# A transformer block on one core: the out-projection and the first two up tiles of the feed-forward, computed in two passes over halves of the tokens

## The chip, the cores and the metric

One core of a Trainium2 chip runs the kernel. The metric is the device time of one execution in microseconds (us); what is given for a kernel is the median of several runs. The core has five engines that run side by side, each through its own list of instructions in order: TensorE (PE, matmuls; PEld are its weight loads), VectorE (DVE), ScalarE (ACT), GpSimd (POOL) and SyncE (SP, which here issues only DMAs). Engines wait for each other by semaphores.

## The reference

Two blocks on a sequence of 1024 tokens of width 1024, all in float32. The part around the change is the end of the first block's mixer and the start of its feed-forward:

```python
mix = jnp.concatenate([attn, rw.astype(x.dtype)], axis=-1) @ w_out[l]
x = x + rms_norm(mix, norm_mix_post[l])
f = conv_gated_ffn(rms_norm(x, norm_ffn_pre[l]), w_ffn_up[l], conv_w[l], conv_b[l], w_ffn_down[l])
x = x + rms_norm(f, norm_ffn_post[l])

def conv_gated_ffn(h, w_up, conv_w, conv_b, w_down):      # w_up: 1024 x 8192, w_down: 4096 x 1024
    u = h @ w_up
    u_pad = jnp.pad(u, ((0, 0), (CONV_WIDTH - 1, 0), (0, 0)))
    u = conv_b + sum(conv_w[j] * u_pad[:, j:j + S] for j in range(CONV_WIDTH))
    gate, val = jnp.split(u, 2, axis=-1)
    return (jax.nn.gelu(gate, approximate=True) * val) @ w_down
```

`rms_norm` divides each token by the root of the mean of its squares over the 1024 channels. So the norm of a token needs all eight channel tiles of the product before it, and two such norms stand one behind the other between the out-projection and the first product of the feed-forward.

## The kernel before

Everything is held with channels on the 128 partitions and tokens along the free axis: a full activation is eight tiles of 128 x 1024 (`KT` = 8, `T` = 1024). A product with a weight tile of 1024 x 128 is `gemm` (line 481): for each of eight k it does three products (high part of the weight by high part of the activation, high by low, low by high), and each of these for both halves of 512 tokens, `hs=(0, 1)`: 48 matmuls of 128x512, into the PSUM banks `2 * u` and `2 * u + 1`. Weight tiles go through two buffers: SP loads tile g into `w_raw`, POOL splits it (`split`, L397 and L400) into `w_hi` and `w_lo` as soon as product g - 2 is done, and PE waits for it (`w_split`).

The out-projection is eight such products (L879 to L887). ACT copies each result to `y1` and squares it; DVE adds the squares in pairs (`norm_pair`), PE sums them over the channels (`norm_part`, L526, matmuls with one output column), ACT takes the root, DVE the reciprocal (`norm_inverse`), and PE spreads it over the partitions (`norm_sum`, L540). DVE then adds the scaled `y1` to the residual `x1`, channel tile by channel tile, ACT squares `x1`, and the second norm runs in the same way. Its result, times a gain, is split into `x_hi` (ACT) and `x_lo` (DVE) by `apply_all`, and the up products of the feed-forward wait for `x_lo` tile by tile (`parts`). Both norms are over all 1024 tokens at once. After them DVE zeroes `f_acc` (L2003), to which the down products of each of the feed-forward's groups are added.

Later, around the feed-forward's own norms, the same kernel already works by halves: `down(h, k)` and `head_tile(h, k)` call `gemm` with `hs=(h,)` (24 matmuls), and `half_sums` (L503), `half_spread` (L511), `half_pair` and `half_inverse` do a norm of 512 tokens. Their rows are shown below.

Nearly every operation of ACT and DVE is issued by the helper at L114, so its line tells little and the names of the tiles have to be read. In the trace digits are cut from the names: `y` is `y1` (or `y2`), `x` is `x1` (or `x2`, `x3`), `x_in` at 1750 us and later is the reloaded `x1`. The order of the work is written out by hand; no scheduler moves it.

## Time and profile before

| | us |
|---|---|
| median of 3 runs | 2678.81 (2676.87 to 2682.08) |
| the profiled execution's own time | 2673.34 |
| its span | 2671.5 |
| PE busy | 2514.2 (94% of the span) |
| DVE busy | 1202.5 (45%) |
| POOL busy | 870.2 (33%) |
| ACT busy | 689.2 (26%) |

The span runs from the first to the last instruction of the profiled execution. Busy times are sums over stages, and 94% on PE says that what can be gained is where PE stands still; that has to be looked up stretch by stretch.

### The profile page before, as it was taken

The page shows a single profiled execution, that of the slowest core. Times are in us where ns is not written, and L with a number is a line of the kernel's source. Part 1 is how long each engine was busy: PE and PEld are TensorE (multiplying, and loading weights), DVE is VectorE, ACT ScalarE, POOL GpSimd, SP SyncE. Part 2 cuts the span into 40 slices and gives each one's busy share as a digit, 9 for nine tenths or more (in the row PEclk, how much of TensorE's full clock was granted, in tenths as well). Part 3 has the DMA queues.
Part 4 walks back from the last instruction along what each step waited for, and adds up shares of the span by engine and source line. Part 5 has one row for each costly group of instructions (what it writes and reads, how often), then busy time and mean ns, then how long its engine had stood idle before and what let it go on. Part 6 is the DMA issues. An engine that isn't in the chain of part 4 may idle for free.

```text
span 2671.5 us, 45354 instructions
## 1 busy us (share of the span) xinstructions
PE 2514.2 (94%) x18246; PEld 2008.6 (75%) x18246; DVE 1202.5 (45%) x1588; ACT 689.2 (26%) x1035; POOL 870.2 (33%) x498
## 2 busy tenths in 40 slices
PE   8999889999879999999999999999979999988897
PEld 6777589986658888888888888877768777733576
DVE  4477766644273422342233223335350666544252
ACT  3233433331222200220022002212332233255521
POOL 3322000011313333344333333465654455400021
PEclk9999989999879999999999999999989999989797
DMA  4211000002122211221122111143311111220021
GB/s 146 70 33 39 22 3 5 4 19 87 40 80 73 75 55 55 72 77 47 63 71 77 48 47 47 47 142 104 128 60 40 50 47 49 75 79 1 0 89 69
DMA packets 44352, 155.98 MB, mean 58 GB/s; under 512 B 4264, under 2 KB 6568, under 8 KB 43688
## 3 DMA queue, kind: packets, MB, share of 16 engines
q1 hardware_dynamic: 26784, 97.53, 11.2%
q10 hardware_dynamic: 17416, 56.31, 6.0%
q8 instruction: 110, 1.80, 0.3%
q14 instruction: 42, 0.34, 0.0%
HBM read 133.37 MB, written 20.45 MB: 58 GB/s over the span
## 4 chain that ended last, share of the span: by engine, by line
PE 83%; DVE 8%; ACT 4%; issue 2%; POOL 1%; DVEq 1%; DMA 0%; ACTq 0%; POOLq 0%
PE ps L493 51%; PE ps L1018 5%; PE ps L598 5%; PE ps L1041 2%; ACT ab L114 2%; DVE proj L114 2%; PE ps L1118 1%; PE ps L762 1%; PE ps L772 1%; DVE x_lo L114 1%; PE ps L547 1%; PE ps L769 1%; DVE nrm_a L114 1%; DVEq L103 1%; PE ps L1138 1%
## 5 line engine op out<-in xcount | busy, mean ns | idle before, releaser
L397 POOL TENSOR_TENSOR w_hi<-w_raw,small 128x1024 fp32r<-128x1024 f32 x178 | 339.3, 1906 | 1494.5 <-PE ps L493 1137.3
L493 PE MATMUL ps<-x_hi,w_hi 128*128 128x512 f32 x1600 | 512.0, 394 | 31.5 <-DVE x_lo L114 15.7
L493 PE MATMUL ps<-x_lo,w_hi 128*128 128x512 f32 x1600 | 507.5, 391 | 0.0
L493 PE MATMUL ps<-x_hi,w_lo 128*128 128x512 f32 x1600 | 507.3, 391 | 0.0
L400 POOL TENSOR_TENSOR w_lo<-w_raw,w_hi 128x1024 fp32r<-128x1024 f32 x178 | 436.4, 2452 | 13.9
L493 PEld LDWEIGHTS ps<-x_hi,w_hi 128*128 128x128 f32 x1600 | 300.2, 189 | 102.4 <-issue 18.5
L493 PEld LDWEIGHTS ps<-x_hi,w_lo 128*128 128x128 f32 x1600 | 302.1, 189 | 63.7
L493 PEld LDWEIGHTS ps<-x_lo,w_hi 128*128 128x128 f32 x1600 | 302.4, 189 | 62.9
L114 DVE SCALAR_TENSOR_TENSOR cv<-ps,cst,cv 128x1023 f32<-128x1023 f32 x64 | 82.1, 1283 | 256.2 <-ACT cv L114 250.8
L493 PE MATMUL ps<-f_hi,w_hi 128*128 128x512 f32 x512 | 170.1, 393 | 3.8 <-POOL w_lo L400 3.8
L493 PE MATMUL ps<-f_hi,w_lo 128*128 128x512 f32 x512 | 168.8, 391 | 0.0
L493 PE MATMUL ps<-f_lo,w_hi 128*128 128x512 f32 x512 | 168.8, 391 | 0.0
L114 DVE TENSOR_TENSOR f_acc<-f_acc,ps 128x1024 f32 (+1 forms) x40 | 40.3, 1008 | 252.7 <-PE ps L493 251.0
L114 ACT ACTIVATE cg<-ps,cst 128x1024 f32<-128x1024 f32 x32 | 38.7, 1210 | 394.3 <-PE ps L493 394.3
L114 DVE SCALAR_TENSOR_TENSOR cg<-ps,cst,cg 128x1023 f32<-128x1023 f32 x64 | 82.1, 1282 | 110.8 <-ACT cg L114 105.0
L114 ACT ACTIVATE cv<-ps,cst 128x1024 f32<-128x1024 f32 x32 | 38.7, 1209 | 306.7 <-PE ps L493 306.7
L493 PEld LDWEIGHTS ps<-f_hi,w_hi 128*128 128x128 f32 x512 | 96.6, 189 | 24.2 <-POOL w_lo L400 4.4
L493 PEld LDWEIGHTS ps<-f_hi,w_lo 128*128 128x128 f32 x512 | 96.5, 189 | 20.4
L493 PEld LDWEIGHTS ps<-f_lo,w_hi 128*128 128x128 f32 x512 | 96.4, 188 | 19.8
L598 PE MATMUL ps<-x_hi,w_hi 128*128 128x512 f32 x224 | 90.7, 405 | 2.7 <-DVE raw L114 2.6
L114 DVE TENSOR_TENSOR zz<-proj,e 128x256 f32<-128x256 f32 x112 | 70.2, 626 | 40.2 <-ACT e L114 28.6
L598 PE MATMUL ps<-x_lo,w_hi 128*128 128x512 f32 x224 | 88.0, 393 | 0.0
(290 smaller groups left out, 3822.0 us busy)
## 6 DMA issues: line engine op xcount, KB each, us to landing
w_raw<-wall SPq DMA_DIRECT2D x178, 512.0 KB, 3.5
ada_w<-wada ACTq DMA_DIRECT2D x24, 512.0 KB, 3.5
fill_spill<-stage ACTq DMA_DIRECT2D x24, 256.0 KB, 2.0
x_in<-xT ACTq DMA_DIRECT2D x8, 512.0 KB, 8.4
x<-xT ACTq DMA_DIRECT2D x1, 4096.0 KB, 12.5
x_spill<-x ACTq DMA_DIRECT2D x1, 4096.0 KB, 11.1
x_in<-x_spill ACTq DMA_DIRECT2D x2, 2048.0 KB, 12.6
x_spill<-x ACTq DMA_DIRECT2D x2, 2048.0 KB, 8.3
```

The source lines that it names most:

```text
L103: self.eng.drain()
L114: return emit(*args, **kw)
L397: nc.gpsimd.tensor_tensor(w_hi[:, u, :, :], w_raw[:, u, :, :], sm["one"].unsqueeze(2).to_broadcast([P, KT, P]), ALU.mult).then_inc(S("w_hi ...
L400: nc.gpsimd.tensor_tensor(w_lo[:, u, :, :], w_raw[:, u, :, :], w_hi[:, u, :, :].bitcast(F32), ALU.subtract).then_inc(S("w_split"), 1)
L493: last = mm(ps[:, 2 * u + h, :], w[:, u, k, :], x[:, k, h * 512:(h + 1) * 512], start=(k == 0 and w is w_hi and x is hi), stop=(k == KT - ...
L547: last = mm(ps[:, b + h, :], w[:, u, k, :], x[:, k, h * 512:(h + 1) * 512], start=(k == 0 and w is w_hi and x is x_hi), stop=(k == KT - 1 ...
L598: last = mm(ps[:, 7, :], w[:, g % 2, k, :], x[:, k, h * 512:(h + 1) * 512], start=(k == 0 and w is w_hi and x is x_hi), stop=(k == KT - 1 ...
L762: last = mm(ps[q, 4 + p, m * RC:(m + 1) * RC], m1[q, r, m, 0:RC], xx[q, r, 0, m, :], start=True, stop=True)
L769: mm(ps[q, 4 + p, m * RC:(m + 1) * RC], xx[q, r, 1, m, :], y_sb[q, p, m, :], start=True, stop=True)
L772: last = mm(ps[q, 4 + p, 256 + m * RC:256 + (m + 1) * RC], y_sb[q, p, m, :], xx[q, r, 1, m, :], start=True, stop=True)
L1018: last = mm(ps[:, 7, :], w[:, g % 2, k, :], x[:, k, h * 512:(h + 1) * 512], start=(k == 0 and w is w_hi and x is x_hi), stop=(k == KT - 1 ...
L1041: i_ = mm(ps[0:r, 2 * (l % 2) + h % 2, (h // 2) * n:(h // 2 + 1) * n], lh, rh, start=True, stop=True)
```

## The change

The out-projection's eight products become sixteen of 24 matmuls: first all eight channel tiles for tokens 0 to 511, then all eight for tokens 512 to 1023 (`out_half`). For this SP loads the eight tiles of `w_out` a second time and POOL splits them a second time (positions 28 to 35; the feed-forward starts at position 36). The two norms between out-projection and feed-forward are done per half, with the helpers that the later stage already used; the norms of half 0 are placed in PE's order between the products of the second pass. The first two up products (the first gate and the first value tile) are also done by halves: `up_half(0, 0)` and `up_half(0, 1)` before the last sums of half 1's norms, `up_half(1, 0)` and `up_half(1, 1)` behind them. Both halves use the same split weights. The spill of `x1` to memory is two DMAs, one per half. The zeroing of `f_acc` goes, and the first group's down products are copied into it instead of added; for that the first group stands outside the loop on PE and DVE. The later stages change in semaphore counts only.

```diff
-G_IN, G_OUT, G_FFN = 0, 20, 28
+G_IN, G_OUT, G_FFN = 0, 20, 36
+W_FFN = G_OUT + KT
 FFN_GROUPS, GROUP = 4, 8
-W_IN2 = G_FFN + FFN_GROUPS * 3 * GROUP
+W_IN2 = W_FFN + FFN_GROUPS * 3 * GROUP
...
+        sq_m = at("sq_m", [P, 2, T], 38)
+        pairs_m = at("pairs_m", [P, 2, T], 40)
...
-            return sq_l[:, k // 2 % 2, :] if lane == "a" else sq_r[:, k // 2 % 2, hc(i % 2)]
+            return sq_l[:, k // 2 % 2, :] if lane == "a" else (sq_m if i < 2 else sq_r)[:, k // 2 % 2, hc(i % 2)]
         def half_pairs(lane, i, j):
-            return pairs_l[:, j % 2, :] if lane == "a" else pairs_a[:, j % 2, hc(i % 2)]
+            return pairs_l[:, j % 2, :] if lane == "a" else (pairs_m if i < 2 else pairs_a)[:, j % 2, hc(i % 2)]
...
-            with sp.Fori(G_OUT // 2, G_LAST // 2) as i:
-                for u in range(2):
-                    g = sp.snap(2 * i + u)
-                    src = dr["wall"][bass.ds(g, 1)]
-                    sp.wait_ge(S("w_split"), 2 * i + u - 1)
-                    load(src, u).then_inc(S(f"w_in{u}"), 16)
+            for lo, hi, back in ((G_OUT, G_OUT + KT, 0), (G_OUT + KT, G_LAST, KT)):
+                with sp.Fori(lo // 2, hi // 2) as i:
+                    for u in range(2):
+                        g = sp.snap(2 * i + u - back)
+                        src = dr["wall"][bass.ds(g, 1)]
+                        sp.wait_ge(S("w_split"), 2 * i + u - 1)
+                        load(src, u).then_inc(S(f"w_in{u}"), 16)
...
-                if k1 == KT:
+                if k1 == KT and whole:
...
+            def out_half(h, k, k0=0, k1=KT):
+                g = G_OUT + KT * h + k
+                gemm(g, g % 2, x_hi, x_lo, parts=("x_lo_done", 8) if h == k == 0 else None, hs=(h,), k0=k0, k1=k1)
+            def up_half(h, u, k0=0, k1=KT):
+                gemm(G_FFN + u, u, x_hi, x_lo, parts=("x_lo_done", 16 + 8 * h), hs=(h,), k0=k0, k1=k1, whole=(h == 1))
             pe.wait_ge(S("inv_used"), 4)
-            gemm(G_OUT, 0, x_hi, x_lo, parts=("x_lo_done", 8))
+            out_half(0, 0)
             pe.wait_ge(S("bonus_used"), 4)
-            gemm(G_OUT + 1, 1, x_hi, x_lo)
-            for k in range(2, KT):
-                gemm(G_OUT + k, k % 2, x_hi, x_lo)
-                if k % 2:
-                    norm_part(1, (k - 3) // 2)
-            norm_sum(1, 3)
-            norm_sum(2)
-            def ffn_up(gr):
-                with pe.Fori(0, GROUP) as j:
+            for k in range(1, KT):
+                out_half(0, k)
+                if k in (2, 4, 6):
+                    half_sums("a", 0, k // 2 - 1)
+            out_half(1, 0, 0, 4)
+            half_sums("a", 0, 3)
+            out_half(1, 0, 4)
+            half_spread("a", 0)
+            out_half(1, 1)
+            half_sums("b", 0, 0)
+            out_half(1, 2)
+            half_sums("b", 0, 1)
+            half_sums("a", 1, 0)
+            out_half(1, 3, 0, 3)
+            half_sums("b", 0, 2)
+            out_half(1, 3, 3)
+            half_sums("b", 0, 3)
+            out_half(1, 4, 0, 3)
+            half_spread("b", 0)
+            out_half(1, 4, 3)
+            out_half(1, 5)
+            half_sums("a", 1, 1)
+            out_half(1, 6)
+            out_half(1, 7, 0, 4)
+            half_sums("a", 1, 2)
+            out_half(1, 7, 4)
+            up_half(0, 0, 0, 4)
+            half_sums("a", 1, 3)
+            up_half(0, 0, 4)
+            half_spread("a", 1)
+            up_half(0, 1)
+            for j in range(KT // 2):
+                half_sums("b", 1, j)
+            half_spread("b", 1)
+            for u in range(2):
+                up_half(1, u)
+            def ffn_up(gr, first=0):
+                with pe.Fori(first, GROUP) as j:
                     g = pe.snap(3 * GROUP * gr + G_FFN + 2 * j)
                     for u in range(2):
...
+            def ffn_down(gr):
...
+            ffn_up(0, 1)
+            ffn_down(0)
+            with pe.Fori(1, FFN_GROUPS - 1) as gr:
+                ffn_up(gr)
+                ffn_down(gr)
...
+            eng.preload_act_table_set("sqrt_and_others")
...
+            def mixed(h, k):
+                g = G_OUT + KT * h + k
+                act.wait_ge(S("gemm_mm"), g + 1)
+                copy(y1[:, k, hc(h)], ps[:, 2 * (g % 2) + h, :]).then_inc(S("gemm_evac"), 1)
+                half_square("a", h, k, y1[:, k, hc(h)])
+            def x1_square(h, k):
+                act.wait_ge(S("res_done"), KT * h + k + 1)
+                half_square("b", h, k, x1[:, k, hc(h)])
+            def x1_spill(h):
+                act.dma_start(x1_dram.rearrange("p (k t) -> p k t", t=T)[:, :, hc(h)], x1[:, :, hc(h)]).then_inc(S("x1_out"), 16)
+            def scaled_high(h, k):
+                act.wait_ge(S("h_done"), 8 * h + k + 1)
+                copy(x_hi[:, k, hc(h)], scaled_bank(h, k)).then_inc(S("x_hi_done"), 1)
             for k in range(KT):
-                g = G_OUT + k
-                act.wait_ge(S("gemm_mm"), g + 1)
-                copy(y1[:, k, :], pair(2 * (g % 2))).then_inc(S("gemm_evac"), 1)
-                act.wait_ge(S("norm_pair"), 4 + k // 2)
-                fn(sq_of[1][:, k % 2, :], y1[:, k, :], ACT.Square).then_inc(S("norm_sq"), 1)
-            root(1)
-            norm(2, lambda k: x1[:, k, :], lambda k: act.wait_ge(S("res_done"), k + 1))
-            act.dma_start(x1_dram, x1[:, :, :].rearrange("p k t -> p (k t)")).then_inc(S("x1_out"), 16)
-            high(1, lambda k: nrm_a[:, k % 2, :], "h_done")
-            act.wait_ge(S("x1_out"), 16)
+                mixed(0, k)
+            half_root("a", 0)
+            for i in range(KT):
+                for k in ((), (0, 1, 2), (3, 4, 5), (6, 7), (), (), (), ())[i]:
+                    x1_square(0, k)
+                if i == 3:
+                    x1_spill(0)
+                if i == 4:
+                    half_root("b", 0)
+                for k in ((), (), (), (), (0, 1, 2), (3, 4, 5, 6), (7,), ())[i]:
+                    scaled_high(0, k)
+                mixed(1, i)
+            half_root("a", 1)
+            for k in range(KT):
+                x1_square(1, k)
+            x1_spill(1)
+            half_root("b", 1)
+            for k in range(KT):
+                scaled_high(1, k)
+            act.wait_ge(S("x1_out"), 32)
...
-            for j in range(4):
-                norm_pair(1, j)
-            norm_inverse(1)
-            dve.wait_ge(*landed("x_again"))
-            for k in range(KT):
-                stt(nrm_a[:, k % 2, :], y1[:, k, :], par("g_mix_post", k, 1), rs_of(1), ALU.mult, ALU.mult)
-                tt(x1[:, k, :], x1[:, k, :], nrm_a[:, k % 2, :], ALU.add).then_inc(S("res_done"), 1)
-                if k >= 2 and k % 2 == 0:
-                    norm_pair(2, k // 2 - 1)
-            norm_pair(2, 3)
-            apply_all(2, 2, nrm_a, lambda k: x1[:, k, :], lambda k: par("g_ffn_pre", k, 1))
-            memset(f_acc[:, 0:8, :], 0.0)
...
+            def mix_residual(h, k):
+                stt(step_bank(h), y1[:, k, hc(h)], par("g_mix_post", k, 1), half_bank("a", h), ALU.mult, ALU.mult)
+                tt(x1[:, k, hc(h)], x1[:, k, hc(h)], step_bank(h), ALU.add).then_inc(S("res_done"), 1)
+            def scaled_up(h, k):
+                stt(scaled_bank(h, k), x1[:, k, hc(h)], par("g_ffn_pre", k, 1), half_bank("b", h),
+                    ALU.mult, ALU.mult).then_inc(S("h_done"), 1)
+            def scaled_low(h, k):
+                dve.wait_ge(S("x_hi_done"), 16 + 8 * h + k + 1)
+                tt(x_lo[:, k, hc(h)], scaled_bank(h, k), x_hi[:, k, hc(h)].bitcast(F32), ALU.subtract)\
+                    .then_inc(S("x_lo_done"), 1)
+            for h in range(2):
+                for j in range(3 if h else 0, 4):
+                    half_pair("a", h, j)
+                half_inverse("a", h)
+                if h == 0:
+                    dve.wait_ge(*landed("x_again"))
+                dve.wait_ge(S("half_bc_a"), h + 1)
+                for k in range(KT):
+                    mix_residual(h, k)
+                    if k in (2, 4, 6):
+                        half_pair("b", h, k // 2 - 1)
+                    if h == 0 and k == 5:
+                        half_pair("a", 1, 0)
+                half_pair("b", h, 3)
+                half_inverse("b", h)
+                dve.wait_ge(S("half_bc_b"), h + 1)
+                for k in range(KT):
+                    scaled_up(h, k)
+                    if k:
+                        scaled_low(h, k - 1)
+                    if h == 0 and k == 3:
+                        half_pair("a", 1, 1)
+                scaled_low(h, KT - 1)
+                if h == 0:
+                    half_pair("a", 1, 2)
...
-            with dve.Fori(0, FFN_GROUPS - 1) as gr:
+            def ffn_group(gr, first=False):
                 memset(pair(4), 0.0)
...
-                        tt(f, f, pair(2 * u), ALU.add).then_inc(S("gemm_evac"), 1)
+                        i_ = vcopy(f, pair(2 * u)) if first else tt(f, f, pair(2 * u), ALU.add)
+                        i_.then_inc(S("gemm_evac"), 1)
...
+            ffn_group(0, first=True)
+            with dve.Fori(1, FFN_GROUPS - 1) as gr:
+                ffn_group(gr)
```

What stands on each engine at the places that matter, as the programs list it. On PE, before, between the last product of the out-projection (its last rows) and the first up product; `pairs_141` and `pairs_140` hold the pair sums of the first and the second norm:

```order
L493 MATMUL ps<-x_lo,w_hi 128x512 x2
L493 MATMUL ps<-x_hi,w_lo 128x512 x2
L526 MATMUL ps<-cst,pairs_141 128x1 [waits norm_pair]
L526 MATMUL ps<-cst,pairs_141 128x1 x7
L526 MATMUL ps<-cst,pairs_141 128x1 [waits norm_pair]
L526 MATMUL ps<-cst,pairs_141 128x1 x7
L540 MATMUL ps<-cst,small 128x128 [waits norm_inv]
L540 MATMUL ps<-cst,small 128x128 x7
L526 MATMUL ps<-cst,pairs_140 128x1 [waits norm_pair]
L526 MATMUL ps<-cst,pairs_140 128x1 x7
```

On PE now, in the second pass, around the end of its third and the start of its fourth product (`pairs_m` holds the pair sums of half 0's second norm, `pairs_l` those of the first norms):

```order
L497 MATMUL ps<-x_hi,w_lo 128x512
L507 MATMUL ps<-cst,pairs_m 128x1 [waits half_pair_b]
L507 MATMUL ps<-cst,pairs_m 128x1 x3
L507 MATMUL ps<-cst,pairs_l 128x1 [waits half_pair_a]
L507 MATMUL ps<-cst,pairs_l 128x1 x3
L497 MATMUL ps<-x_hi,w_hi 128x512 [waits gemm_evac,w_split]
L497 MATMUL ps<-x_lo,w_hi 128x512
L497 MATMUL ps<-x_hi,w_lo 128x512
```

The sums of the norms have moved from behind the product of all eight tiles to between products of the second pass, and each still waits for DVE's pair sum. The end of half 1's second norm, with the first up product of half 1 behind it, reads on PE:

```order
L507 MATMUL ps<-cst,pairs_m 128x1 [waits half_pair_b]
L507 MATMUL ps<-cst,pairs_m 128x1 x3
L515 MATMUL ps<-cst,small 128x128 [waits half_inv_b]
L515 MATMUL ps<-cst,small 128x128 x3
L497 MATMUL ps<-x_hi,w_hi 128x512 [waits x_lo_done,gemm_evac,w_split]
L497 MATMUL ps<-x_lo,w_hi 128x512
L497 MATMUL ps<-x_hi,w_lo 128x512
L497 MATMUL ps<-x_hi,w_hi 128x512 [waits x_lo_done]
```

Here PE has nothing left to do but these rows: what it did without a norm has been put ahead of them.

On DVE, before, where the first norm's reciprocal leads into the residual:

```order
L114 RECIPROCAL small<-small 128x8 [waits norm_root]
L114 SCALAR_TENSOR_TENSOR nrm_a<-y_100,cst,ps 128x1024 [waits in_a,norm_bc]
L114 TENSOR_TENSOR x_101<-x_101,nrm_a 128x1024
L114 SCALAR_TENSOR_TENSOR nrm_a<-y_100,cst,ps 128x1024
L114 TENSOR_TENSOR x_101<-x_101,nrm_a 128x1024
```

The same place on DVE now, of half 1:

```order
L115 RECIPROCAL small<-small 128x4 [waits half_root_a]
L115 SCALAR_TENSOR_TENSOR ps<-y_102,cst,ps 128x512 [waits half_bc_a]
L115 TENSOR_TENSOR x_103<-x_103,ps 128x512
L115 SCALAR_TENSOR_TENSOR ps<-y_102,cst,ps 128x512
L115 TENSOR_TENSOR x_103<-x_103,ps 128x512
```

The operations are half as wide, there are twice as many, and the step between the two of a pair lies in PSUM (`ps`) instead of SBUF (`nrm_a`).

## Rows read from the trace of the kernel before

**Rows 1.** The page: the span, and section 1 (busy us, share, instructions).

```profile
span 2671.5 us, 45354 instructions
PE 2514.2 (94%) x18246; PEld 2008.6 (75%) x18246; DVE 1202.5 (45%) x1588; ACT 689.2 (26%) x1035; POOL 870.2 (33%) x498
```

**Rows 2.** Stretches: from:to, length, PE, PEld, DVE, ACT, POOL busy; PEclk, DMA, GB/s.

```profile
624.50:715.60 91.10, 91.08 (x419) 75.97 (x419) 16.19 (x8) 17.20 (x18) 30.06 (x14) 1.00 0.24 87
715.60:765.30 49.70, 23.43 (x111) 22.12 (x111) 32.48 (x27) 14.46 (x15) 4.23 (x2) 0.54 0.16 63
765.30:770.60 5.30, 5.27 (x12) 3.64 (x12) 4.98 (x4) 2.12 (x2) 0.00 (x0) 0.50 0.70 300
796.00:1746.00 950.00, 949.71 (x4200) 786.11 (x4200) 314.44 (x252) 145.17 (x129) 374.35 (x175) 1.00 0.19 61
1757.00:1793.00 36.00, 36.00 (x176) 30.22 (x175) 6.98 (x11) 3.98 (x7) 25.71 (x12) 1.00 0.31 98
```

**Rows 3.** Timeline of PE, 755 to 796: start, duration, what, [idle before <- releaser].

```profile
755.03 3.57 PE L526 MATMUL ps<-cst,pairs 128*128 128x1 f32 x16 [1.45 <-DVE pairs L114]
759.20 1.97 PE L540 MATMUL ps<-cst,small 128*128 128x128 f32 x8 [0.60 <-DVE small L114]
765.33 1.19 PE L493 MATMUL ps<-x_hi,w_hi 128*128 128x512 f32 x2 [4.16 <-DVE x_lo L114]
...
796.01 0.74 PE L493 MATMUL ps<-x_hi,w_hi 128*128 128x512 f32 x2 [0.73 <-DVE cg L114]
```

**Rows 4.** Timeline of PE in the half-width stage: sums, and spread.

```profile
1762.17 0.95 PE L503 MATMUL ps<-cst,pairs_l 128*128 128x1 f32 x8
...
1793.18 0.60 PE L511 MATMUL ps<-cst,small 128*128 128x128 f32 x4
```

**Rows 5.** Timeline of DVE in the half-width stage.

```profile
1762.37 0.69 DVE L114 TENSOR_TENSOR f_acc<-f_acc,ps 128x512 f32<-128x512 f32 x1 [3.97 <-PE ps L493]
1768.76 0.69 DVE L114 TENSOR_TENSOR f_acc<-f_acc,ps 128x512 f32<-128x512 f32 x1 [5.71 <-PE ps L493]
...
1793.45 0.69 DVE L114 TENSOR_TENSOR f_acc<-f_acc,ps 128x512 f32<-128x512 f32 x1 [2.48 <-PE ps L493]
...
1799.29 0.69 DVE L114 TENSOR_TENSOR f_acc<-f_acc,ps 128x512 f32<-128x512 f32 x1 [1.55 <-PE ps L493]
...
1857.42 0.76 DVE L114 SCALAR_TENSOR_TENSOR ps<-f_acc,cst,ps 128x512 f32<-128x512 f32 x1 [3.53 <-PE ps L511]
1858.26 0.69 DVE L114 TENSOR_TENSOR x<-x_in,ps 128x512 f32<-128x512 f32 x1
1859.04 0.76 DVE L114 SCALAR_TENSOR_TENSOR ps<-f_acc,cst,ps 128x512 f32<-128x512 f32 x1
```

**Rows 6.** Timeline of DVE, 628 to 785.

```profile
628.54 2.54 DVE L114 TENSOR_TENSOR x_lo<-proj,x_hi 128x1024 fp32r<-128x1024 f32 x2
...
717.77 3.31 DVE L114 TENSOR_TENSOR pairs<-sq_a 128x1024 f32<-128x1024 f32 x1 [20.24 <-ACT sq_a L114]
...
763.96 1.22 DVE L114 TENSOR_TENSOR x_lo<-nrm_a,x_hi 128x1024 fp32r<-128x1024 f32 x1
...
766.64 1.22 DVE L114 TENSOR_TENSOR x_lo<-nrm_a,x_hi 128x1024 fp32r<-128x1024 f32 x1
...
784.47 6.88 DVE L114 MEMSET f_acc<- 128x8192 f32 x1 [1.83 <-issue]
```

**Rows 7.** Timeline of ACT in the half-width stage: an eviction, a square.

```profile
1864.25 0.60 ACT L114 ACTIVATE proj<-ps 128x512 f32<-128x512 f32 x1 [3.06 <-PE ps L493]
...
1866.50 0.63 ACT L114 ACTIVATE sq_r<-x 128x512 f32<-128x512 f32 x1
```

**Rows 8.** Timeline of POOL: a split after the out-projection, one in the half-width stage.

```profile
717.66 2.34 POOL L400 TENSOR_TENSOR w_lo<-w_raw,w_hi 128x1024 fp32r<-128x1024 f32 x1
...
1774.31 1.90 POOL L397 TENSOR_TENSOR w_hi<-w_raw,small 128x1024 fp32r<-128x1024 f32 x1 [1.13 <-PE ps L493]
1776.28 2.39 POOL L400 TENSOR_TENSOR w_lo<-w_raw,w_hi 128x1024 fp32r<-128x1024 f32 x1
```

**Rows 9.** Tile `w_raw`, 1740 to 1762, beside two reloads of 2 MB each: its DMAs.

```profile
DMA to landing us min/median/max: 3.5/6.3/6.8
```

More of the change, by code:

```diff
@@ L46 @@
 N_POS = G_OUT2 + KT
-WALL_OF = (2 * [G_LAST + k for k in range(KT)] + 2 * [W_IN2 + i for i in IN2_ORDER[:N_HEAD]]
+WALL_OF = (2 * [W_IN2 - KT + k for k in range(KT)] + 2 * [W_IN2 + i for i in IN2_ORDER[:N_HEAD]]
            + [W_IN2 + i for i in IN2_ORDER[N_HEAD:]] + [W_OUT2 + k for k in range(KT)])
@@ L479, in _, with gemm @@
             turned = nc.tensor.transpose
-            def gemm(g, u, hi, lo, first=False, parts=None, hs=(0, 1), k0=0, k1=KT):
+            def gemm(g, u, hi, lo, first=False, parts=None, hs=(0, 1), k0=0, k1=KT, whole=True):
                 if k0 == 0:
@@ L532, in norm_part, with norm_sum @@
                 last.then_inc(S("norm_mm"), 1)
-            def norm_sum(n, done=0):
-                for j in range(done, KT // 2):
+            def norm_sum(n):
+                for j in range(KT // 2):
                     norm_part(n, j)
@@ new lines, in _ @@
+            out_half(1, 5)
[9 more added lines that the diff above has]
+            up_half(0, 1)
+            for j in range(KT // 2):
+                half_sums("b", 1, j)
+            half_spread("b", 1)
+            for u in range(2):
+                up_half(1, u)
@@ L914, in head_tile @@
                 g = G_IN2 + N_HEAD * h + k
[L915 removed]
+                gemm(g, g % 2, x_hi, x_lo, parts=("x_lo_done", 32 + 8 * h) if k == 0 else None, hs=(h,), k0=k0, k1=k1)
             down(0, 0, 0, 7)
@@ L951, in _ @@
             head_tile(0, 1, 0, 1)
-            half_sums("a", 1, 3)
+            half_sums("a", 3, 3)
             head_tile(0, 1, 1, 6)
-            half_spread("a", 1)
+            half_spread("a", 3)
             head_tile(0, 1, 6)
@@ L1169, in _ @@
             g0 = G_OUT2
-            gemm(g0, g0 % 2, x_hi, x_lo, parts=("x_lo_done", 40))
+            gemm(g0, g0 % 2, x_hi, x_lo, parts=("x_lo_done", 48))
             gemm(g0 + 1, (g0 + 1) % 2, x_hi, x_lo)
@@ L1750, in low @@
                 tt(x_lo[:, k, :], src, x_hi[:, k, :].bitcast(F32), ALU.subtract).then_inc(S("x_lo_done"), 1)
-            def apply(n, k, buf, src, gain, shift=None):
-                i_ = stt(buf[:, k % 2, :], src(k), gain(k), rs_of(n), ALU.mult, ALU.mult)
-                if shift is not None:
-                    i_ = ts(buf[:, k % 2, :], buf[:, k % 2, :], shift(k), None, ALU.add)
-                i_.then_inc(S("h_done"), 1)
-            def apply_all(n, n_set, buf, src, gain, shift=None):
-                norm_inverse(n)
-                for k in range(KT):
-                    apply(n, k, buf, src, gain, shift)
-                    if k:
-                        low(n_set, k - 1, buf[:, (k - 1) % 2, :])
-                low(n_set, KT - 1, buf[:, (KT - 1) % 2, :])
             for k in range(KT):
```

156 lines of the change are left out of this document (74 added, 82 removed).

## The prediction

> **What bounds the kernel now.** I read the page first: PE is busy for 94% of the span, no other engine for half of it [rows 1], so the end is set by PE and what can be won is its idle time. The table of stretches shows where that lies. In the out-projection (624.5 to 715.6) PE is full at the full clock, then come 49.7 us in which its 23.4 busy us are only the small matmuls of two norms, at a granted clock of 0.54, and from 796 to 1746, through the feed-forward, PE is full again (949.7 of 950 us) [rows 2]. So nothing behind 796 has slack: what is taken out between 624.5 and 796.0, a window of 171.5 us, comes off the span. The timelines of PE and DVE show the hole from inside: PE waits for DVE, which goes through eight scaled residual tiles and eight normed tiles; the first up product starts at 765.33, released by `x_lo`, and is fed by DVE at 2.68 us per k (763.96 to 766.64); and the third up tile starts at 796.01 after a last wait for DVE, which had been zeroing `f_acc` for 6.88 us [rows 3, 6].
>
> **Unit costs.** A half-width product has a row of its own in the later stage: DVE's evictions there stand 6.39 us apart (1762.37 to 1768.76) with one `half_sums` in between, whose row is 0.95, so 5.44 us for 24 matmuls; with one `half_spread` in between they stand 5.84 apart, so the spread costs PE 0.40 in its stream [rows 4, 5]. Full width costs twice 5.44 for 48 matmuls (91.1 us of the first stretch, less three sums of about 1.7, over eight tiles, gives 10.8 to 10.9) [rows 2], so halving itself costs PE nothing. On DVE one residual tile of 512 tokens takes 1.62 (1857.42 to 1859.04), a pair sum 0.69 and a gap of 0.08; on ACT an eviction 0.60 and a square 0.63 [rows 5, 7].
>
> **The sum, from the first matmul at 624.5, called 0.**
> 1. Sixteen half products: 16 x 5.44 = 87.0, as before.
> 2. The first product now reaches k = 6 and 7 sooner than DVE has written `x_lo`: the last of it is there at 628.54 + 2.54 = 631.08, then three matmuls follow. It ends at 631.8, or 7.3, not 5.44: +1.9 [rows 6].
> 3. Eleven sums stand in the two passes (three of half 0's first norm in pass one, one more of it, four of half 0's second norm, three of half 1's first norm in pass two): 11 x 0.95 = 10.5. Two spreads: 0.8. Walking DVE and ACT through pass two with the unit costs, the spread of half 0's first norm is out at 55.3, its residual is done at 71.2, its second spread is out at 79.2 and its last `x_lo` at 93.0, all ahead of what PE asks for in its order but once: the first sum of the second norm is wanted at 60.5 and its pair is ready at 60.8. +0.4. Pass two ends at 100.6.
> 4. The two up products of half 0, one sum and one spread: 10.9 + 0.95 + 0.4 = 12.2, to 112.8. These cover the start of half 1's norm: eviction and square (1.3) and pair (0.7) are done by 102.7, PE takes the sum at 103.3, and the spread is out at 107.6.
> 5. From there PE is bound by DVE. Eight residual tiles and three pairs: 8 x 1.62 + 3 x 0.77 = 15.3, to 122.9. Last square and pair, with handovers: 1.5, to 124.4. Then sums, root, reciprocal, spread and two multiplies. At full width that stretch took 763.96 - 755.03 = 8.93, of which sums 3.57, spread 1.97 and two multiplies 2.56, so 0.83 for the rest [rows 3, 6]. At half width and the same low clock: 1.79 + 0.99 + 2 x 0.76 + 0.83 = 5.1, to 129.5, where the first `x_lo` begins; PE starts at 130.3, after 17.5 us without a product.
> 6. The product of half 1 is fed by DVE at 0.76 + 0.69 + 2 x 0.08 = 1.61 per k: six of these, 0.8 for the last `x_lo` and 0.7 for three matmuls, to 141.4. The second one: 5.44, to 146.8.
> 7. The third up tile needs the first one's convolution by ACT and DVE, which starts at 141.4, and its own split (1.90 + 2.39 from 141.4, done at 145.8 [rows 8]). DVE is no longer zeroing, ACT has a table load and a DMA issue to get through first. I take 0.5, to 147.3.
>
> So 171.5 - 147.3 = 24.2 us saved. For the profiled execution that is 2673.3 - 24.2 = 2649.1 (span 2671.5 - 24.2 = 2647.3). The median of the runs shown stands 5.5 above the profiled execution, so I predict 2678.8 - 24.2 = 2654.6, rounded to 2655.
>
> **Edits costed at nothing.** Loading and splitting `w_out` twice: POOL's split is 4.37 us with its gap against 5.44 us per product, and in the later stage, which has this very rhythm, POOL waits 1.13 for PE and not the reverse [rows 8]. A load must land within 2 x 5.44 - 4.4 = 6.5 us; beside other transfers of 4 MB loads took 3.5 to 6.8 [rows 9], so at the worst a split starts 0.3 late against a margin of about 1. If that cover goes, each product waits for its split. The copy in place of the add, and the lost zeroing: DVE is idle two thirds of the feed-forward [rows 2]; only the wait at 796.01 was exposed, and step 7 has it. The root's table load moves from the idle stretch to the start of pass one, where the bank that it delays is needed again only 5.4 us later. The spill of `x1` in two parts is waited for only behind all of step 6. The first group outside the loop adds code; no row shows what fetching costs, between nothing and one wait like that at 796.01, 1 us; I take nothing, since no fetch delays PE in rows 2's 950 us.
>
> **The unknown sizes.** The clock: after the idle stretch the first twelve matmuls took 5.3 us at a granted clock of 0.50, the lower of the two levels (1.2 GHz), where 12 x 0.227 = 2.7 would do [rows 2]. In the changed kernel that low stretch falls under DVE's pace if it passes during `up_half(1, 0)` (three low matmuls, 1.3, are shorter than 1.61), and costs up to 2.6 if it runs into `up_half(1, 1)`. It could also not fall at all, then steps 5 and 6 are 1.2 shorter. I take the low clock for the norm and the full one for the last product. DVE's chain with more small waits than in rows 5: 0 to 1. Stalls in pass two: 0 to 3. Step 7: 0 to 1.5.
>
> **A rule on the shared port.** The pair sum at 717.77 took 3.31 us where its like takes 1.22, while POOL wrote `w_lo` until 720.00 [rows 6, 8]: a DVE operation held back by POOL by 2.1 us. The Trainium skill says so too (SBUF — State Buffer, "Who interferes with whom"): a DVE instruction with two SBUF inputs contends with a GpSimd instruction that reads SBUF, and the loser is blocked for the whole instruction. By that rule the new operations, each of which has one of its two tensor inputs in PSUM, are free; the half-width rows, 0.69 and 0.76 beside a POOL that is at work 25.7 of 36 us, agree [rows 2, 5]. Without that protection a residual tile could be held in every split, which is the first rival.
>
> **Rivals.**
> - *Stalls in pass two.* PE's sums stand in its order and block all matmuls behind them. If DVE falls behind, by being held 2.1 us per 5.44 or because ACT, which also evicts the products in order, delays the squares, half 0's 38 us of DVE chain grow to about 50, and PE loses some 12. Saved 12: 2667. For: the chain of half 0 ends only 4 to 7 us ahead of its last use in steps 3 and 4, and ACT's evictions and squares are interlocked with DVE's pairs. Against: the operands are in PSUM, and the later stage with the same helpers shows PE busy 36.0 of 36.0 [rows 2].
> - *Slower than before.* POOL does not keep the pace of half products. To eat the 24.2 us each of the 14 products behind the first two would have to wait 1.7 us for its split, a rhythm of 7.2; from there on it is a loss, and at 7.6 it stands at 2685. For it speaks only that splits now come twice as often while 4 MB of `x1` arrive; against, the waits of POOL for PE at that rhythm [rows 8].
> - *More than forecast.* The clock stays up, no wait in pass two, no wait at step 7: 1.2 + 0.4 + 0.5, and the first product's wait is partly covered, 1 more; with luck on DVE's gaps 28 saved: 2651.
>
> **Chances and range.** Forecast 0.70, stalls 0.16, more 0.09, slower 0.05. The forecast's own range is saved 20 to 27, 2652 to 2659, with about 3 us to either side for what medians of three differ by (2676.87 to 2682.08 shown). The range of 8 in 10 reaches into the stalls: 2648 to 2667. 0.2% is 5.4 us, about what a measurement of this kernel can tell from no change. Faster by more: the forecast, the gain above it and nearly all of the stalls, 0.93; within 0.2%: 0.03, from deeper stalls; slower: 0.04.
>
> **What would show it.** In the profile after: evictions `y<-ps` of 128x512 every 5.44 us or 6.39 with a sum, POOL ahead of PE by about 1 us throughout; one idle stretch of PE of about 17 us (with small sums in it) where there were 50; `x_lo` of half 1 at 1.6 us per k; the third up tile about 147 us after the first matmul of the out-projection; from there on the same length to the end as before. I am wrong if PE waits for pairs or `w_lo` by more than 3 us in pass two, if half-width operations of DVE take 2 us and more beside POOL, or if the feed-forward behind it gets longer.

## The result and the profile after

| | before | changed |
|---|---|---|
| median, first measurement (6 runs each) | 2677.84 (2673.06 to 2683.59) | 2658.61 (2649.07 to 2661.43) |
| ratio, its 95% interval | | 0.9924 (0.9902 to 0.9945) |
| median, second measurement (17 and 6 runs) | 2680.76 (2672.83 to 2685.01) | 2655.04 (2650.48 to 2661.31) |
| ratio, its 95% interval | | 0.9905 (0.9885 to 0.9924) |
| span of the profiled execution | 2671.5 | 2659.5 |
| first matmul of the out-projection to third up tile | 171.49 | 148.54 |

The changed kernel is faster, by 0.76 and 0.95% in the two measurements; the medians lie 19.2 and 25.7 us apart. The forecast was 2655 within 2648 to 2667.

The page says little by itself: PE busy goes from 94% to 95%. POOL's row changed most, from 870.2 to 904.6 us for the eight further splits [rows 1]:

```profile
span 2659.5 us, 45576 instructions
PE 2520.2 (95%) x18246; PEld 2006.5 (75%) x18246; DVE 1195.6 (45%) x1629; ACT 694.3 (26%) x1069; POOL 904.6 (34%) x514
```

The table of stretches of the changed kernel (from:to, length, PE, PEld, DVE, ACT, POOL busy, granted clock, DMA share, GB/s) shows what became of the hole of 49.7 us [rows 2]: two passes of the out-projection, the up products of half 0, one wait, the up products of half 1, and the feed-forward:

```profile
629.00:731.10 102.10, 99.86 (x481) 82.64 (x482) 37.24 (x50) 32.35 (x52) 64.33 (x30) 1.00 0.39 135
731.10:743.40 12.30, 12.29 (x60) 9.93 (x59) 5.74 (x9) 3.33 (x6) 4.28 (x2) 1.00 0.24 80
743.40:760.80 17.40, 7.77 (x36) 7.04 (x37) 11.84 (x19) 4.52 (x8) 0.00 (x0) 0.58 0.31 121
760.80:777.50 16.70, 15.13 (x48) 9.93 (x49) 12.82 (x16) 6.08 (x8) 4.30 (x2) 0.82 0.11 31
777.50:1727.50 950.00, 949.63 (x4201) 786.02 (x4200) 314.88 (x252) 145.71 (x129) 375.01 (x175) 1.00 0.20 62
```

One wait of 17.4 us is left. Inside it, the timeline of PE (start, duration, what, [idle before <- releaser]) has the second norm of half 1 and the first up product of half 1, which answer to [rows 3]:

```profile
737.32 0.60 PE L515 MATMUL ps<-cst,small 128*128 128x128 f32 x4
...
743.60 1.05 PE L507 MATMUL ps<-cst,pairs_m 128*128 128x1 f32 x8 [0.21 <-DVE pairs_m L115]
747.67 1.87 PE L507 MATMUL ps<-cst,pairs_m 128*128 128x1 f32 x8 [3.02 <-DVE pairs_m L115]
751.73 1.87 PE L507 MATMUL ps<-cst,pairs_m 128*128 128x1 f32 x8 [2.20 <-DVE pairs_m L115]
754.70 1.87 PE L507 MATMUL ps<-cst,pairs_m 128*128 128x1 f32 x8 [1.09 <-DVE pairs_m L115]
757.13 1.11 PE L515 MATMUL ps<-cst,small 128*128 128x128 f32 x4 [0.57 <-DVE small L115]
760.82 0.77 PE L497 MATMUL ps<-x_hi,w_hi 128*128 128x512 f32 x1 [2.57 <-DVE x_lo L115]
```

And the timeline of DVE at the same place, which answers to [rows 5, 6]:

```profile
734.93 0.18 DVE L115 RECIPROCAL small<-small 128x4 f32<-128x4 f32 x1 [1.80 <-ACT small L115]
737.96 0.76 DVE L115 SCALAR_TENSOR_TENSOR ps<-y,cst,ps 128x512 f32<-128x512 f32 x1 [2.85 <-PE ps L515]
738.79 0.69 DVE L115 TENSOR_TENSOR x<-x,ps 128x512 f32<-128x512 f32 x1
739.57 0.76 DVE L115 SCALAR_TENSOR_TENSOR ps<-y,cst,ps 128x512 f32<-128x512 f32 x1
...
758.28 1.60 DVE L115 SCALAR_TENSOR_TENSOR ps<-x,cst,ps 128x512 f32<-128x512 f32 x2 [1.21 <-PE ps L515]
759.98 0.69 DVE L115 TENSOR_TENSOR x_lo<-ps,x_hi 128x512 fp32r<-128x512 f32 x1
760.76 0.76 DVE L115 SCALAR_TENSOR_TENSOR ps<-x,cst,ps 128x512 f32<-128x512 f32 x1
```

The reciprocal of half 1's first norm is ready at 735.11, but PE comes to the spread only at 737.32, behind the whole first up product of half 0. Then DVE walks 1.61 us per tile. PE has nothing left of half 0, and its granted clock goes down (0.58 on average over these 17.4 us): the second to fourth sum take 1.87 where the first took 1.05.

**The stretch and the span do not agree, and why.** From here on "the stretch" is the time from PE's first matmul of the out-projection to its first matmul of the third up tile. In the changed kernel these two are:

```profile
629.01 0.50 PE L497 MATMUL ps<-x_hi,w_hi 128*128 128x512 f32 x1 [1.37 <-DVE proj L115]
...
777.55 0.62 PE L497 MATMUL ps<-x_hi,w_hi 128*128 128x512 f32 x2
```

The stretch is 22.95 us shorter, the span of these two profiled executions only 12.0. The rest lies where the change did nothing: the out-projection began at 629.0 instead of 624.5, and the second block's stick-breaking stage (its attention over earlier tokens, late in the span) took 5.3 us longer. Further profiles of the same two kernels show that this is how executions differ. The kernel before began the out-projection at 624.52 and at 628.79, the changed one at 629.01, 624.73, 627.42 and 627.81; the second block's stick-breaking stage (from the reload of the gates, `gate_a`, to the reload of x2) took 224.5 and 224.0 in the kernel before, and 229.8, 229.8, 223.6 and 229.8 in the changed one. The stretches of that stage of the changed kernel's third and fourth profile, in the columns of above:

```profile
2319.10:2542.70 223.60, 187.05 (x698) 97.22 (x699) 97.90 (x180) 118.47 (x163) 0.00 (x0) 0.89 0.06 24
```

```profile
2319.90:2549.80 229.90, 196.43 (x698) 100.99 (x699) 97.92 (x180) 118.50 (x163) 0.00 (x0) 0.85 0.06 23
```

The same 698 matmuls, the same busy time on DVE and ACT, but a granted clock of 0.89 in one and 0.85 in the other, and 6.3 us between them. So a change of 20 us in 2660 is read from the stretch that it touches (148.54, 148.31, 148.55 and 148.22 in the four profiles; 171.49 and 171.47 before), and the median only has to agree.

That the stretch is gained in full behind it can be read too. From the third up tile to the first reload of `x1` at the end of the feed-forward (`x_in<-x_spill`, issued by ACT) it is 945.7 to 945.9 us in every profile of this document but one, the zeroing put back (948.6). And from the first matmul of the out-projection to the reload of the gates it is 1714.1 and 1715.4 us in the two profiles before, and 1691.7 to 1692.3 in the four of the changed kernel.

### The profile page after: what moved, and what is told of

It reads as the page before. It is cut to its first block, busy times and chain, and to the rows that moved or that the text cites. A ratio compares the mean times of both kernels' runs of the same rounds, so it can differ in the third digit from the quotient of the medians.

```text
span 2659.5 us, 45576 instructions
## 1 busy us (share of the span) xinstructions
PE 2520.2 (95%) x18246; PEld 2006.5 (75%) x18246; DVE 1195.6 (45%) x1629; ACT 694.3 (26%) x1069; POOL 904.6 (34%) x514
## 4 chain that ended last, share of the span: by engine, by line
PE 83%; DVE 6%; issue 4%; ACT 4%; POOL 1%; DMA 1%; DVEq 0%; ACTq 0%; POOLq 0%; SPq 0%
PE ps L497 51%; PE ps L1063 5%; PE ps L602 5%; PE ps L1086 2%; ACT ab L115 2%; PE ps L1163 2%; PE ps L766 1%; PE ps L776 1%; PE ps L551 1%; PE ps L773 1%; DVE proj L115 1%; PE ps L507 1%; DVE x_lo L115 1%; POOL w_lo L404 1%; DMA w_raw<-wall 1%
## 5 line engine op out<-in xcount | busy, mean ns | idle before, releaser
L401 POOL TENSOR_TENSOR w_hi<-w_raw,small 128x1024 fp32r<-128x1024 f32 x186 | 354.5, 1906 | 1447.7 <-PE ps L497 1082.9
L497 PE MATMUL ps<-x_hi,w_hi 128*128 128x512 f32 x1600 | 527.3, 395 | 28.8 <-DVE x_lo L115 13.0
L497 PE MATMUL ps<-x_lo,w_hi 128*128 128x512 f32 x1600 | 520.8, 391 | 0.0
L497 PE MATMUL ps<-x_hi,w_lo 128*128 128x512 f32 x1600 | 520.4, 391 | 0.0
L404 POOL TENSOR_TENSOR w_lo<-w_raw,w_hi 128x1024 fp32r<-128x1024 f32 x186 | 455.6, 2449 | 14.6
L497 PEld LDWEIGHTS ps<-f_hi,w_hi 128*128 128x128 f32 x512 | 96.8, 189 | 24.2 <-POOL w_lo L404 4.4
L115 DVE TENSOR_TENSOR f_acc<-f_acc,ps 128x1024 f32 (+1 forms) x32 | 30.6, 955 | 186.4 <-PE ps L497 185.3
L602 PE MATMUL ps<-x_hi,w_hi 128*128 128x512 f32 x224 | 91.0, 406 | 2.7 <-DVE raw L115 2.6
L421 POOL COPY xx<-rmask 128x512 f32<-128x512 f32 x16 | 9.7, 615 | 239.7 <-PE ps L799 179.4
```

The lines of the kernel that those rows point to most:

```text
L115: return emit(*args, **kw)
L401: nc.gpsimd.tensor_tensor(w_hi[:, u, :, :], w_raw[:, u, :, :], sm["one"].unsqueeze(2).to_broadcast([P, KT, P]), ALU.mult).then_inc(S("w_hi ...
L404: nc.gpsimd.tensor_tensor(w_lo[:, u, :, :], w_raw[:, u, :, :], w_hi[:, u, :, :].bitcast(F32), ALU.subtract).then_inc(S("w_split"), 1)
L497: last = mm(ps[:, 2 * u + h, :], w[:, u, k, :], x[:, k, h * 512:(h + 1) * 512], start=(k == 0 and w is w_hi and x is hi), stop=(k == KT - ...
L602: last = mm(ps[:, 7, :], w[:, g % 2, k, :], x[:, k, h * 512:(h + 1) * 512], start=(k == 0 and w is w_hi and x is x_hi), stop=(k == KT - 1 ...
```

## The experiments

Each is read by the stretch just defined, and by the ratio of its time to that of the kernel before.

### The changed kernel again

No edit.

> The changed kernel once more, for a second profile and more runs. Theory: the stretch from the first matmul of the out-projection to the third up tile is fixed by the program and stays at 148.5 us within 0.5; what lies ahead of it and behind it (629.0 and 1882.0 us in the first profile of the change, against 624.5 and 1875.5 before it) moves by several us from one execution to the next with the clock granted in the attention stages, and has nothing to do with the change. The median of the time comes out 22 to 24 us below the kernel before. Rival: the change itself makes the stages around it 11 us longer (more code, more semaphore traffic), then both stretches come out as long as in its first profile, and the gain is 12 to 19 us.

Measured: stretch 148.31; ratio 0.9905 (0.9885 to 0.9924), 25.7 us between the medians; span 2655.1. It began at 624.7, so the first of the two differences was gone, but the stick-breaking stage took 229.8 again. Two more single profiles of it, and one of the kernel before, were taken for that, without an edit.

> The changed kernel, a third profile. In the first two the second block's attention stage (from the reload of the gates to the reload of x2) took 229.8 us, in the kernel before 224.5 and 224.0. Theory: its length goes with the granted clock of that stage (0.85 against 0.87 to 0.89) and varies from one execution of the same kernel to the next, so a profile of the changed kernel with 222 to 225 us will be found. Rival: it is fixed at 229.8 by the change, and the profiles' gain is 6 us less than the stretch tells.

> The changed kernel, a fourth profile, for the same question: 222 to 225 or 229.8 us in the second block's attention stage.

> The kernel before once more, for a second profile. Theory: the stretch from the first matmul of the out-projection to the third up tile is again 171.5; the stretches ahead of and behind it differ from the first profile by several us with the granted clock. Rival: they are fixed (624.5 and 1875.5), and what moved in the profiles of the changed kernel is then the change's doing.

Measured: 223.6 in the third (span 2651.0), 229.8 in the fourth (span 2658.1). The kernel before, again: stretch 171.47 (628.79 to 800.26), stage 224.0, span 2676.5. One kernel gives both lengths; the rival, that the change fixes it at 229.8, has fallen. The six kernels of the sections below that differ from the changed one had 222.4 to 225.4 us, and so had the kernel before without the zeroing (223.9). It stays open why three of four profiles of the changed kernel itself had the longer one. When the stage begins does not sort them: it began at 2317.04 in a profile with 229.8 and at 2316.78 in one with 223.6 (the clock kept up).

### The zeroing put back

```diff
                 if h == 0:
                     half_pair("a", 1, 2)
+            memset(f_acc[:, 0:8, :], 0.0)
             dve.sem_inc(S("prod"), 1)
```

> The changed kernel with the zeroing of f_acc put back in its old place, behind the last x_lo; the rest unchanged (the first group still copies). Theory: before the change the 6.88 us of zeroing cost only the 0.95 us by which the third up tile came late, since a whole full-width product stood between; now only a half product of 5.4 us does, so it delays the first convolution on DVE and the third up tile by 5.3 us: stretch 153.9, time up by about 5. Rival: it costs what it cost before, 1 us, since it is the same instruction at the same place.

Measured: stretch 155.93, 7.4 more than in the first profile of the change, where 5.3 was expected; ratio to the kernel before 0.9929 (0.9907 to 0.9951), against 0.9905 for the changed kernel in the same session. DVE, and PE behind it:

```profile
770.83 6.88 DVE L115 MEMSET f_acc<- 128x8192 f32 x1 [1.83 <-issue]
778.04 0.91 DVE L115 MEMSET ps<- 128x1024 f32 x1 [0.33 <-issue]
779.34 1.28 DVE L115 SCALAR_TENSOR_TENSOR cg<-ps,cst,cg 128x1023 f32<-128x1023 f32 x1 [0.38 <-issue]
```

```profile
782.13 1.22 PE L497 MATMUL ps<-x_hi,w_hi 128*128 128x512 f32 x2 [6.66 <-DVE cg L115]
783.16 1.05 PE L497 MATMUL ps<-x_lo,w_hi 128*128 128x512 f32 x2
784.01 1.05 PE L497 MATMUL ps<-x_hi,w_lo 128*128 128x512 f32 x2
```

PE now waits 6.66 us for the first convolution, and what I had not counted: after that wait the first 13 matmuls run 0.43 us apart instead of 0.23, at the low clock, so the product itself is 2.8 us longer (from its start to ACT's first step of the next convolution 14.1 us, against 11.3). The zeroing costs 10 us here by this count, of which only the wait was expected. The later mark agrees: from the first matmul of the out-projection to the reload of the gates it is 1702.2 us, 10 more than in the changed kernel. The medians of the session lie 7.4 us apart and the ratios 0.0024, which is 6.4 us, with intervals that overlap.

### The kernel before without the zeroing

The edit of the changed kernel's feed-forward (`ffn_group`, first group outside the loop, copy for add, no `memset`) made in the kernel before, and nothing else.

```diff
-            memset(f_acc[:, 0:8, :], 0.0)
...
-                        tt(f, f, pair(2 * u), ALU.add).then_inc(S("gemm_evac"), 1)
+                        i_ = vcopy(f, pair(2 * u)) if first else tt(f, f, pair(2 * u), ALU.add)
+                        i_.then_inc(S("gemm_evac"), 1)
```

> The kernel before with one part of the change alone: no zeroing of f_acc, the first group of the feed-forward outside the loop on DVE and copied instead of added. Theory: only the 0.95 us by which the third up tile came late can go, so the stretch from the first matmul of the out-projection to the third up tile falls from 171.5 to 170.5 and the time is not measurably different. Rival, from the 6.7 us that the zeroing costs in the changed kernel: the same instruction costs the same here, stretch 165, time down by 6.

Measured: the third up tile starts at 795.23, without a wait, 170.59 after 624.64, so the stretch is 0.9 us shorter, as the theory said:

```profile
794.77 0.62 PE L493 MATMUL ps<-x_hi,w_lo 128*128 128x512 f32 x2
795.23 0.62 PE L493 MATMUL ps<-x_hi,w_hi 128*128 128x512 f32 x2
```

The ratio came out at 0.9977 (0.9963 to 0.9991), 2 to 10 us: more than the stretch tells. The profile's span is 2671.0 against 2671.5 and 2676.5 for the two of the kernel before, and from the out-projection to the gates it is 1714.0 against 1714.1 and 1715.4. I cannot attribute the rest; it is of the size by which stages elsewhere differed between executions above.

The same 6.88 us thus cost 0.9 us in one order and 10 in the other. The part of the change that drops the zeroing is worth next to nothing alone. Together with the halving it is worth a third of the stretch's gain (7.4 of 23.0), and 2.8 us more behind the stretch.

### The first two up tiles at full width

```diff
-            up_half(0, 0, 0, 4)
             half_sums("a", 1, 3)
-            up_half(0, 0, 4)
             half_spread("a", 1)
-            up_half(0, 1)
...
-            for u in range(2):
-                up_half(1, u)
+            for u in range(2):
+                gemm(G_FFN + u, u, x_hi, x_lo, parts=("x_lo_done", 24))
```

> The changed kernel with the first two up tiles done at full width behind both halves' norms (the out-projection still in two passes). Theory: the half products of half 0 fill a wait of PE and would be worth their 10.9 us, but they also hold up the spread of half 1's first norm by 2.5 us, and without them the first full-width product hides its second half under DVE's pace of 1.6 us per k, in part at the low clock: the stretch grows by about 5 us, to 153.5. Rival: the full 10.9 us, to 159.4.

Measured: stretch 153.75 (third up tile at 782.71, start 628.96), 5.2 more; ratio 0.9914 (0.9892 to 0.9936). The two half products of half 0 do 10.9 us of PE's work in the wait and are worth half of it. The trace says where the other half goes. Without them PE comes to half 1's norm sooner, and the first up product starts 129.9 us after the out-projection instead of 131.8. It takes 13.0 us at full width against 11.3 for half 1 alone, since the half product spends part of its time waiting for DVE (1.63 us per k) and the full one, behind its first wait, none, though its first matmuls run at the low clock (about ten, 0.43 us apart). The second takes 10.9 against 5.4. That is 1.7 and 5.4 more, less 1.9: 5.2.

### Half 0's norm without its cover

PE: the sums and spreads of half 0, except those of its first norm's squares, moved behind the second pass; ACT and DVE in the matching order.

```diff
             out_half(1, 0, 4)
-            half_spread("a", 0)
             out_half(1, 1)
...
-            half_sums("b", 0, 0)
...
-            half_spread("b", 0)
...
             out_half(1, 7, 4)
+            half_spread("a", 0)
+            for j in range(KT // 2):
+                half_sums("b", 0, j)
+            half_spread("b", 0)
...
+            for k in range(KT):
+                x1_square(0, k)
+            x1_spill(0)
+            half_root("b", 0)
+            for k in range(KT):
+                scaled_high(0, k)
```

> Two passes and norms by halves as in the changed kernel, but half 0's spread, residual and second norm stand behind the second pass instead of under it (PE's sums of it, ACT's and DVE's parts moved with them). Theory: the gain is that cover and nothing else; without it the two halves' chains run one after the other with only the two up products of half 0 between: stretch about 176 us, 27.5 more than the changed kernel and 4.6 more than the kernel before (171.5). Rival: halving the steps already pipelines the chain over the engines, and the stretch lies between 150 and 165.

Measured: stretch 178.76, 30.2 more than the changed kernel and 7.3 more than the kernel before; the ratio is 1.0023 (1.0010 to 1.0035), slower than before by 3 to 9 us. On PE two rows of holes follow each other, here the first product after each:

```profile
745.02 0.76 PE L497 MATMUL ps<-x_hi,w_hi 128*128 128x512 f32 x1 [2.57 <-DVE x_lo L115]
...
786.62 0.76 PE L497 MATMUL ps<-x_hi,w_hi 128*128 128x512 f32 x1 [2.57 <-DVE x_lo L115]
```

So halving does nothing for the chain by itself: half-width operations take 0.69 and 0.76 us instead of 1.23 and 1.28, but there are twice as many, and the fixed parts (sums, root, reciprocal, spread) come twice. Taking half 0's norm out from under the second pass costs 30.2 us, more than the whole gain of 23.0.

### The clock kept up

```diff
+            def keep(n):
+                for m in range(n):
+                    mm(ps[:, 3, :], w_hi[:, 1, m % KT, :], x_hi[:, m % KT, 0:512], start=True, stop=True,
+                       skip_group_check=True)
             for j in range(KT // 2):
                 half_sums("b", 1, j)
+                keep((12, 12, 8, 4)[j])
             half_spread("b", 1)
+            keep(9)
```

> The changed kernel with 45 more matmuls of 128x512 whose result is not used (into a bank that is free then), between and behind the sums of half 1's second norm: 12, 12, 8, 4 and 9. They fill PE's wait for DVE so that the granted clock has no reason to fall. Theory: the last sum takes 0.95 instead of 1.87 and the spread 0.60 instead of 1.11, both on the chain, so the stretch falls by 1.4 us to 147.1; the up product of half 1 stays at DVE's 1.63 us per k. Rival: the clock costs nothing, since PE only waits, and the extra matmuls stand in front of the sums: stretch 148.5 to 151.

Measured: stretch 148.10 (772.61 - 624.51), ratio 0.9886 (0.9869 to 0.9902). PE's sum and spread at the end of the chain:

```profile
750.78 1.05 PE L507 MATMUL ps<-cst,pairs_m 128*128 128x1 f32 x8
751.70 1.17 PE L925 MATMUL ps<-x_hi,w_hi 128*128 128x512 f32 x4
752.71 0.60 PE L515 MATMUL ps<-cst,small 128*128 128x128 f32 x4
753.06 2.33 PE L925 MATMUL ps<-x_hi,w_hi 128*128 128x512 f32 x9
```

The sum went from 1.87 to 1.05 and the spread from 1.11 to 0.60, but the stretch gained only 0.1 to 0.45 on the four profiles of the changed kernel, where 1.4 was expected. Part of that is another wait: the split of the third product was late by 1.36 us in this execution and by 0.59 in the second profile of the changed kernel. Counted from the same point behind it (half 1's first pair sum of the second norm), the first product of half 1 starts 1.0 us earlier than there. The low clock in the wait costs only what stands on the chain within it: the sums and the spread, not the matmuls that wait for DVE anyway. The ratio is lower than the stretch explains; this execution had the stick-breaking stage at 223.6 us.

### The spread earlier, the reload in two parts

```diff
-            up_half(0, 0, 4)
+            up_half(0, 0, 4, 6)
             half_spread("a", 1)
+            up_half(0, 0, 6)
             up_half(0, 1)
...
-            act.dma_start(x1[:, :, :], dr["xT"].rearrange("p (k t) -> p k t", t=T)).then_inc(landed("x_again")[0], 16)
+            act.dma_start(x1[:, :, hc(0)], dr["xT"].rearrange("p (k t) -> p k t", t=T)[:, :, hc(0)])\
+                .then_inc(landed("x_again")[0], 16)
...
                 mixed(0, k)
+                if k == 3:
+                    act.dma_start(x1[:, :, hc(1)], dr["xT"].rearrange("p (k t) -> p k t", t=T)[:, :, hc(1)])\
+                        .then_inc(S("x_again_1"), 16)
```

> The changed kernel with two small moves: half 1's first spread stands behind k = 5 of the first up product of half 0 instead of behind k = 7, and x1 is reloaded by two DMAs of 2 MB, the second one issued behind the fourth product of pass one. Theory: the reciprocal was ready 2.2 us before PE came to the spread, so half 1's chain starts 1.4 us earlier; and the split that waited 3.7 us for its weight tile beside the 4 MB reload comes in time, which saves the 0.6 to 1.3 us of PE's wait: stretch 146.3. Rival: the loads are late for another reason (the queue, not the reload), then only the 1.4: 147.1.

Measured: stretch 146.17 (775.41 - 629.24), where 146.3 was expected, and no wait of PE for `w_lo` in it (the slowest load landed after 6.8 us); ratio 0.9875 (0.9857 to 0.9893), median 2649.55 (2645.81 to 2650.59).

### All three

The edits of the last two sections together; on PE:

```diff
+            up_half(0, 0, 6)
             up_half(0, 1)
...
                 half_sums("b", 1, j)
+                keep((12, 12, 8, 4)[j])
             half_spread("b", 1)
+            keep(9)
```

> Both moves of the early spread and the split reload together with the 45 filling matmuls. Theory: the gains add, 1.4 + 0.8 + 1.4, stretch 144.9, the time 3.6 us below the changed kernel and 27 below the kernel before. Rival: the filling matmuls hold up sums that now come at other times; stretch not below 146.

Measured: stretch 145.11 (770.15 - 625.04), ratio 0.9885 (0.9869 to 0.9902), median 2650.81 (2647.63 to 2651.60). The stretch comes out within 0.2 of the 144.9 that was expected, and 1.06 below the version without the filling matmuls, which agrees with the 1.0 counted above. In the median it can't be told from that version, which is simpler and the one to keep.

## Why the prediction was right, step by step

The stretch was forecast at 147.3 and is 148.5; the saving 24.2, measured 23.0 in the stretch and 19.2 and 25.7 between medians. The difference of 1.2 in the stretch is 1.5 too little in step 3, 0.2 too little in step 6 and 0.5 too much in step 7.

- Steps 1 and 2, half products at 5.44 and the late `x_lo`: the first product waited 0.91 and 0.35 us at k = 6 and 7 and the next began at 7.4, forecast 7.3. Right. (The check of the 5.44 against the first stretch is slightly off: 91.1 less three sums of 1.7, over eight, is 10.75 and not 10.8 to 10.9. Nothing else rests on it.)
- Step 3, end of pass two: forecast 100.6, measured 102.1. PE stopped for three reasons in the passes. Two had been forecast, the late `x_lo` of step 2 and a pair sum (0.20, where 0.4 was said). The third was costed at nothing: POOL's split of a tile waited 3.68 us for its load, and PE 0.77 for POOL (1.36 at the most in the other profiles); the evictions on either side of it stand 6.51 apart instead of 5.44, so it took 1.07 of the 1.5. PE and POOL, in the profile of the change, and the line on the DMAs of `w_raw` from 636 to 680:

```profile
654.66 0.50 PE L497 MATMUL ps<-x_hi,w_hi 128*128 128x512 f32 x1 [0.77 <-POOL w_lo L404]
```

```profile
650.26 1.90 POOL L401 TENSOR_TENSOR w_hi<-w_raw,small 128x1024 fp32r<-128x1024 f32 x1 [3.68 <-DMA w_raw<-wall]
652.23 2.38 POOL L404 TENSOR_TENSOR w_lo<-w_raw,w_hi 128x1024 fp32r<-128x1024 f32 x1
```

```profile
DMA to landing us min/median/max: 3.3/3.5/8.9
```

  I had bounded a load beside another transfer by 6.8 us [rows 9]. Issued 5.6 us behind one reload of 4 MB it took 8.9, over the 6.5 that the rhythm leaves. The mechanism was named and its size was short by 2 us. With the reload in two parts the wait for `w_lo` was gone (slowest load 6.8 and 6.0 us in the two profiles).
- Step 4: 12.2 forecast, 12.3 measured; the spread of half 1's first norm was out at 108.9 instead of 107.6, late by what step 3 had lost.
- Step 5, the chain on DVE: from spread to the first product of half 1 22.7 us forecast (107.6 to 130.3), 22.9 measured (737.96 to 760.82). POOL stands idle through all of it (735.6 to 772.4), so the rule on the shared port is not tested here but under the second pass, where half 0's norm runs beside the splits:

```profile
685.11 1.90 POOL L401 TENSOR_TENSOR w_hi<-w_raw,small 128x1024 fp32r<-128x1024 f32 x1 [1.98 <-PE ps L497]
687.08 2.41 POOL L404 TENSOR_TENSOR w_lo<-w_raw,w_hi 128x1024 fp32r<-128x1024 f32 x1
```

```profile
686.40 0.69 DVE L115 TENSOR_TENSOR x<-x,ps 128x512 f32<-128x512 f32 x1
687.18 0.76 DVE L115 SCALAR_TENSOR_TENSOR ps<-y,cst,ps 128x512 f32<-128x512 f32 x1
688.01 0.69 DVE L115 TENSOR_TENSOR x<-x,ps 128x512 f32<-128x512 f32 x1
```

  From 685 to 724 every such operation, each with one tensor in PSUM, took 0.69 to 0.76 (0.80 in the row of two), beside POOL or not, and none was held; that bears out what the Trainium skill says (SBUF — State Buffer, "Who interferes with whom") for this case. Half 0's chain took 38.0 us from its first spread to its last `x_lo`, as forecast (55.3 to 93.0), so the first rival had nothing to stand on.
- Step 6: 11.1 and 5.44 forecast, 16.7 together measured. The low clock ended during the first half product of half 1 at 766.6 (matmuls 0.43 us apart up to there and 0.23 behind it), under DVE's pace, as taken.
- Step 7: 0.5 forecast, 0 measured. The convolution of the first up tile was done at 776.66, 0.9 us ahead of need. That it was close is what the zeroing shows: put back, it costs 10 us.
- The rivals: no stall in pass two beyond 0.2 us; POOL kept the rhythm of 5.44 except once; the "more than forecast" one did not come, its waits of DVE in the chain being real.
- What the forecast missed is not in its sum but in its weights: I treated the dropped zeroing as worth the one wait at 796.01 that it had caused (0.73 us [rows 3]). Alone it is worth 0.9, and 10 us in the company of the half-width up products, which leave half as long until the first convolution is needed. The sum was right because it priced the new order without the zeroing, not because the part had been priced.

## What to carry to other kernels

Here the two-pass order paid only through what is placed under the second pass: without that cover the same halving was 7 us slower than the kernel before. When a pass gets shorter, look again at everything that was hidden behind its old length, since one memset went from 0.9 to 10 us. And where stages elsewhere move by 6 us from one execution to the next, judge a small change by the stretch that it touches, in more than one profile.

## What was not expected of the hardware

- A weight load of 512 KB took 8.5 to 9.5 us behind one reload of 4 MB, in all eight profiles that had it in this place. Beside two DMAs of 2 MB elsewhere it had taken 6.8 at the most, and 3.3 to 3.5 alone. In the kernel before, where it was issued 9.2 us behind the same reload instead of 5.6, it took 4.5. That the overlap with the reload decides is likely by these numbers, and not tested by itself.
- After a wait of 6.66 us the product behind it ran its first 13 matmuls 0.43 us apart instead of 0.23 and lost 2.8 us more, so this wait of PE cost 1.4 times its length.
- One stage with the same 698 matmuls took 223.6 or 229.8 us in different executions of one kernel, at a granted clock of 0.89 or 0.85. What decides between them stays open.
